# Seven half-size products in place of eight for the down projections of two feed-forward blocks, and the first weight slabs among the sums of the first norm

## The chip, the cores and the metric

The kernel is one program on one NeuronCore of a Trainium2 chip. All data is f32. The metric is the device time of one launch in microseconds; the median of three runs is given. TensorE multiplies, VectorE and ScalarE work on the results, SyncE asks for the weights, and the four run in parallel, held in order by semaphores only.

## The reference

Two transformer blocks over 256 latent tokens beside 256 context tokens, width 1024. The first has window pooling, differential attention, a bidirectional RWKV recurrence and a mixture of 32 experts. The second has two layers, each an attention mixer and a SwiGLU feed-forward of width 2816. What the change touches is the last line of each layer, and the first lines of the first block:

```
s = silu(c); mod = s @ w_ada + b_ada            # 6 x 1024 rows: shift, scale, gate, twice
p = (rms_norm(x, norm1_g) * (1 + scale) + shift) @ w_in

def swiglu(h, w_gate_up, w_down):
    g, u = split(h @ w_gate_up, 2)               # h: tokens x 1024, g and u: tokens x 2816
    return (silu(g) * u) @ w_down                # w_down: 2816 x 1024
h_lat = h_lat + g_f * swiglu(modulate(h_lat, sh_f, sc_f), w_gate_up, w_down)
h_ctx = h_ctx + cg_f * swiglu(...)               # first of the two layers only
```

The first layer (named "f0" in the kernel) sends 512 tokens through its feed-forward, the second ("f1") 256.

## The kernel before, in words

**Layout.** Features lie on the 128 partitions, tokens along them: the residual `H` and the normed activations `A` are 8 tiles of 128 x 512. A product takes a 128 x 128 unit of weights as the stationary operand and streams tokens past it into one of 8 PSUM banks (`banks`, 128 x 512). Every f32 matmul leaves two records in the profile, so counts of records are twice the counts in the code.

**Weights.** SyncE (`straight`, L2189) copies the weight stream from HBM to a ring of six 1 MB tiles of 16 units. It asks for tile t once TensorE has finished with tile t - 6. TensorE waits for a tile when it takes its first unit (`unit`). The tables, the parameters and the tokens are asked for from ScalarE's queue.

**Feed-forward, gate and up (`ffn`).** Both halves of the weights and tokens are cut in two, and each of 22 hidden tiles is computed as seven half-size products of four matmuls (the Winograd form of Strassen's scheme), 28 matmuls of 128 x 256 in f0 and of 128 x 128 in f1. VectorE makes the four sums of weight blocks for the tile after (`weights_summed`: four operations of 128 x 512, two buffers `wsum`), the four sums of token blocks once (`tsums`), and combines the products; ScalarE copies and applies silu. After the last hidden tile TensorE waits for VectorE's last product with silu (L2163).

**Feed-forward, down (`ffn_down`).** Eight output tiles in order. Each is one PSUM group of 22 matmuls, over all tokens at once (512 columns in f0, 256 in f1), read straight from the ring and from `hid`. VectorE adds the finished bank to the residual (`residual`, L1931 and L1933 in f0, L1937 in f1).

**Norm (`norm`).** ScalarE squares the eight tiles of `H`, each once its residual is there (L1289). TensorE sums them over the partitions with a matrix of ones in four strips (L530), ScalarE takes the root, VectorE the reciprocal (L1599), TensorE spreads the result to all partitions, and VectorE multiplies (L1604 in the first norm, L1613 in later ones).

**Start.** ScalarE asks for the parameters, for `ident` and `ones`, for the tokens (2 MB, `x_in`) and for the other tables (1.5 MB, `tables_in`). SyncE starts the weights when the tokens are there. TensorE transposes the tokens, does norm n1, then the first eight modulation slabs (`modulation`: one 1 MB tile each, four matmuls of 128 x 32 by 128 x 512 in four column strips, eight records a slab), turns the result (`modulation_out`, L542), and VectorE makes the coefficients (L1581, L1590, L1593). ScalarE then applies them to the normed tiles (L1307), and the first projection follows tile by tile. Between the root of n1 and the slabs' copy ScalarE asks for two small tables, `sw` (1.2 MB) and `cnt` (0.6 MB).

## Time and profile before

| | us |
|---|---|
| median of 3 runs | 2477.55 (2477.21 to 2479.27) |
| the profiled execution | 2481.53 |
| its span | 2479.7 |
| TensorE busy | 2315.2 (93% of the span) |
| VectorE busy | 909.7 (37%) |
| ScalarE busy | 497.2 (20%) |
| mean granted TensorE clock | 0.963 of full speed |

The span runs from the first to the last instruction that the profiler shows; the execution's own time is 1.8 us longer. In all rows times are in us from the span's start unless ns is written, "x" is a count of records, and what stands in square brackets is the idle time of that engine just ahead of the row, with what ended it.

### The profile page before, as it was taken

How to read it: one execution, taken by the hardware profiler on the slowest of the kernel's cores; microseconds unless marked ns; L12 is line 12 of the kernel's file. 1: busy time of each engine (PE TensorE's matmuls, PEld its weight loads, DVE VectorE, ACT ScalarE, POOL GpSimd, SP SyncE). 2: the span in 40 equal slices, each digit the busy share in tenths (PEclk: the TensorE clock that was granted, in tenths of full speed). 3: DMA queues.
4: the chain of work that ended last, by engine and by line, in shares of the span. 5: the costliest groups of instructions: out<-in, count | busy, mean ns of one | idle time of the engine just before them, and what ended most of it. 6: DMA issues, size and time to landing. Idle time of an engine off the chain costs nothing.

```text
span 2479.7 us, 40905 instructions
## 1 busy us (share of the span) xinstructions
PE 2315.2 (93%) x17296; PEld 1534.1 (62%) x17296; DVE 909.7 (37%) x1966; ACT 497.2 (20%) x1057; POOL 0.2 (0%) x4
## 2 busy tenths in 40 slices
PE   6999866999899899999999989999999999799998
PEld 3554415999788444444444437658888445688997
DVE  1047677444212221212123027444444001457731
ACT  3010342332002111111112026411010001251111
POOL 0000000000000000000000000000000000000000
PEclk8999987999899999999999999999999999999998
DMA  8253793000543699999982210012222122113431
GB/s 347 86 221 154 309 415 159 4 4 4 199 163 131 283 422 422 422 421 422 422 355 119 85 68 1 18 53 96 89 85 85 51 88 103 52 36 142 166 142 60
DMA packets 59638, 428.00 MB, mean 173 GB/s; under 512 B 6496, under 2 KB 7776, under 8 KB 8288
## 3 DMA queue, kind: packets, MB, share of 16 engines
q1 hardware_dynamic: 56880, 414.21, 42.2%
q10 hardware_dynamic: 2608, 11.58, 1.2%
q8 instruction: 120, 1.97, 0.3%
q14 instruction: 30, 0.25, 0.0%
HBM read 424.72 MB, written 1.05 MB: 172 GB/s over the span
## 4 chain that ended last, share of the span: by engine, by line
PE 89%; DVE 7%; ACT 1%; DMA 1%; issue 1%; ACTq 0%; DVEq 0%
PE bank L530 86%; PE bank L677 1%; DMA ring<-in_w 1%; DVE normed L1613 1%; DVE arena L1818 0%; ACT normed L1307 0%; DMA arena<-in_xin 0%; PE bank L1144 0%; DVE arena L1682 0%; DVE arena L1681 0%; DVE arena L1734 0%; PE bank L1153 0%; DVE arena L1830 0%; DVE arena L1829 0%; DVE small L1649 0%
## 5 line engine op out<-in xcount | busy, mean ns | idle before, releaser
L530 PE MATMUL bank<-arena 64*64 64x64 f32 (+8 forms) x8808 | 811.0, 291 | 22.2 <-DVEq L471 12.9
L530 PEld LDWEIGHTS bank<-arena 64*64 64x64 f32 (+4 forms) x8808 | 576.1, 150 | 212.2 <-issue 173.2
L530 PE MATMUL bank<-normed,ring 128*128 128x256 f32 (+2 forms) x1984 | 545.4, 432 | 15.2 <-DVE normed L1632 5.5
L530 PEld LDWEIGHTS bank<-normed,ring 128*128 128x128 f32 x1984 | 356.0, 195 | 192.9 <-issue 151.8
L530 PE MATMUL bank<-arena,ring 128*128 128x256 f32 (+2 forms) x1376 | 363.3, 420 | 4.6 <-DVE arena L2163 3.1
L530 PEld LDWEIGHTS bank<-arena,ring 128*128 128x128 f32 x1376 | 249.1, 190 | 111.3 <-issue 84.4
L530 PE MATMUL bank<-ring,arena 128*64 128x512 f32 (+1 forms) x1008 | 208.4, 611 | 6.2 <-DMA ring<-in_w 4.0
L530 PEld LDWEIGHTS bank<-ring,arena 128*64 128x64 f32 (+1 forms) x1008 | 62.8, 133 | 140.4 <-issue 120.8
L530 PE MATMUL bank<-ring,normed 128*32 128x512 f32 (+2 forms) x576 | 115.7, 606 | 19.9 <-DMA ring<-in_w 12.1
L1534 ACT ACTIVATE arena<-arena 128x256 f32<-128x256 f32 (+1 forms) x88 | 32.1, 365 | 341.4 <-DVE arena L2160 216.4
L2050 DVE TENSOR_TENSOR arena<-arena,bank 128x512 f32<-128x512 f32 x72 | 49.5, 688 | 136.9 <-PE bank L530 136.8
L530 PEld LDWEIGHTS bank<-ring,normed 128*32 128x32 f32 (+1 forms) x576 | 41.7, 141 | 80.9 <-issue 50.4
L1289 ACT ACTIVATE arena<-resid 128x512 f32<-128x512 f32 (+1 forms) x48 | 25.2, 524 | 322.8 <-DVE resid L1933 197.5
L1931 DVE SCALAR_TENSOR_TENSOR resid<-bank,mod2a,resid 128x256 f32<-128x256 f32 x16 | 7.7, 483 | 194.6 <-PE bank L530 194.6
L1334 ACT ACTIVATE arena<-bank,small 128x512 f32<-128x512 f32 (+1 forms) x112 | 69.1, 622 | 48.5 <-DVE small L1649 47.7
L1649 DVE TENSOR_REDUCE small<-bank 128x1 f32<-128x512 f32 (+1 forms) x112 | 63.8, 609 | 37.8 <-PE bank L530 37.7
L530 PE MATMUL bank<-arena,con 128*32 128x128 f32 (+6 forms) x640 | 68.7, 309 | 8.8 <-ACT arena L1289 3.4
L530 PEld LDWEIGHTS bank<-arena,con 128*32 128x32 f32 (+2 forms) x640 | 42.2, 138 | 37.6 <-issue 22.0
L530 PE MATMUL bank<-normed,arena 128*128 128x256 f32 (+1 forms) x352 | 64.8, 327 | 0.0
L1868 DVE TENSOR_TENSOR arena<-arena,bank 128x256 f32<-128x256 f32 x80 | 33.7, 421 | 79.9 <-PE bank L530 79.8
L1315 ACT ACTIVATE arena<-bank 128x512 f32<-128x512 f32 (+1 forms) x38 | 19.3, 508 | 207.5 <-PE bank L530 207.5
L530 PE MATMUL bank<-arena,sw 128*64 128x128 f32 (+4 forms) x288 | 50.5, 393 | 9.2 <-DVE arena L2095 9.2
(309 smaller groups left out, 1663.8 us busy)
## 6 DMA issues: line engine op xcount, KB each, us to landing
ring<-in_w SPq DMA_DIRECT2D x296, 1024.0 KB, 7.9
arena<-in_w SPq DMA_DIRECT2D x99, 1024.0 KB, 11.3
arena<-in_xin ACTq DMA_DIRECT2D x1, 2048.0 KB, 8.3
arena<-in_nab ACTq DMA_DIRECT2D x1, 2048.0 KB, 11.4
con<-in_con ACTq DMA_DIRECT2D x1, 1472.5 KB, 11.3
sw<-in_sw ACTq DMA_DIRECT2D x1, 1280.0 KB, 5.8
sw<-in_sw ACTq DMA_DIRECT2D x1, 1168.0 KB, 8.4
normed<-in_xin ACTq DMA_DIRECT2D x1, 1024.0 KB, 5.7
```

The costliest lines, as they stand in the source:

```text
L530: return nc.tensor.matmul(o, l, r, start=start, stop=stop, **kw)
L677: last = nc.tensor.transpose(banks[j[0]][:, c * P:(c + 1) * P], it["p"][x][:, c * P:(c + 1) * P], ident)
L1289: a.signals(f(sq[:, k, 0:n], H[:, k, cols], ACT.Square), "squared_" + name)
L1315: a.given(f(o, view(b, o), ACT.Copy, scale=scale))
L1334: a.given(f(it["p"][x][:, 0:it["nk"]], b[:, 0:it["nk"]], ACT.Exp, bias=it["nm"][:, x:x + 1], accum_out=it["den"][:, x:x + 1]))
L1534: f(z[:, half, :], z[:, half, :], ACT.Silu).then_inc(S("gate_silu_" + name), 1)
L1613: ins = tt(A[:, k, cols], H[:, k, cols], spread[:, 0:n], MUL)
L1649: ins = V.tensor_reduce(nm[:, x:x + 1], b[:, 0:nk], AX, MAX, negate=True)
L1868: v.gives(tt(SC[d]["Pt"], SC[d]["Pt"], j4(b, 256), ADD))
L1931: stt(out=H[:, k, 0:CTX], in0=b[:, 0:CTX], scalar=m[:, c + 1:c + 2], in1=H[:, k, 0:CTX], op0=MUL, op1=ADD)
L2050: v.given(tt(y, y, b[:, :], ADD))
```

## The change

The down product is cut as gate and up already are. The 22 hidden tiles are two halves of 11, the tokens two halves, and two output tiles form a pair, so a pair is a 2 x 2 block product done as seven products over 11 hidden tiles instead of eight. The 11 are taken in three parts of 4, 4 and 3 (`DOWN`), each with its own 1 MB weight tile (12 tiles a block, where there were 11; the last of three is padded); the seven sums stay open in seven banks over the three parts. VectorE makes the weight sums of every part, the sums of hidden blocks in the first pair (`hidden_summed`), and from the seven banks of a pair the four residual additions (`add_pair`). The norms behind both blocks wait for pairs, and put their squares into `A`.

At the start, five of the eight modulation slabs are put among the strips' sums of n1, behind its tiles 1, 3, 5, 6 and 7 (`first_slab`); the wait for the tables moves behind the first projections; and the tables, `cnt` and `sw` are asked for behind the copy of the modulation rows.

```diff
+FH = FT // 2
+DOWN = [range(lo, min(lo + 4, FH)) for lo in range(0, FH, 4)]
+N_FFN = FT * 2 * KD + KD // 2 * len(DOWN) * UPT
...
+        hsums = {n: [region(o, FH * n // 2, "p (f t) -> p f t", f=FH) for o in (11264, 14080, 22528)] for n in (T, SEQ)}
+        usums = {n: [region(16896 + n // 2 * i, n // 2) for i in range(5)] for n in (T, SEQ)}
...
                 for k in range(KD):
                     pe.wait_ge(S("squared_" + name), k + 1)
                     last = sums(k, (2, 3) if halves else range(4))
-                done(j, last)
+                    if k == KD - 1:
+                        done(j, last)
+                    if each is not None:
+                        each(k)
...
             def ffn_down(n, name):
-                marks["res_" + name] = dict(gave)
-                for m in range(KD):
-                    j = job("dve")
-                    for f in range(FT):
-                        last = mm(banks[j[0]][:, 0:n], unit(), hid[:, f, 0:n], f == 0, f == FT - 1)
-                    done(j, last)
+
+                q = n // 2
+                marks["down_" + name] = []
+                x11, x21, t3, x22 = (lambda k, lo=lo, c=c: hid[:, lo + k, c * q:(c + 1) * q]
+                                     for lo, c in ((0, 0), (FH, 0), (0, 1), (FH, 1)))
+                t1, t2, t4 = (lambda k, z=z: z[:, k, :] for z in hsums[n])
+                tile = FT
+                for m in range(KD // 2):
+                    js = [None] * 7
+                    for part, ks in enumerate(DOWN):
+                        w = unit(UPT)
+                        final = part == len(DOWN) - 1
+                        if final:
+                            st["free"][-1] = st["n"] + 7
+                        a = lambda i, h, k: w[:, (8 * i + 4 * h + k) * P:(8 * i + 4 * h + k + 1) * P]
+                        s1, s2, s3, s4 = (lambda k, z=z: z[:, k * P:(k + 1) * P] for z in wsum[tile % 2])
+                        for x, (l, r, weights, tokens) in enumerate((
+                                (lambda k: a(0, 0, k), x11, 0, 0), (lambda k: a(0, 1, k), x21, 0, 0), (s4, x22, 3, 0),
+                                (s2, t2, 1, 2), (s3, t3, 2, 3), (s1, t1, 1, 1), (lambda k: a(1, 1, k), t4, 0, 4))):
+                            if part == 0:
+                                js[x] = job("dve")
+                            if weights:
+                                pe.wait_ge(S("weights_summed_" + name), 3 * tile + weights)
+                            if tokens and m == 0:
+                                pe.wait_ge(S("hidden_summed_" + name), 4 * part + tokens)
+                            for k in ks:
+                                last = mm(banks[js[x][0]][:, 0:q], l(k - ks[0]), r(k), k == 0, k == FH - 1)
+                            if final:
+                                done(js[x], last)
+                        if not final:
+                            last.then_inc(full, 1)
+                            st["n"] += 1
+                        marks["down_" + name].append(st["n"])
+                        tile += 1
...
             transposes_in(xtok, None, "x_in")
-            norm("n1", sq_t, slice(0, T))
-            pe.wait_ge(S("silu_c"), 1)
             st["banks"] = 7
-            for x in range(KD):
+
+            def first_slab(k):
+
+                if k in (1, 3, 5, 6, 7):
+                    y = {1: 0, 3: 1, 5: 2, 6: 3, 7: 4}[k]
+                    if y == 0:
+                        pe.wait_ge(S("silu_c"), 1)
+                    modulation(y, ADA, cond1)
+
+            norm("n1", sq_t, slice(0, T), each=first_slab)
+            for x in range(5, KD):
                 modulation(x, ADA, cond1)
             modulation_out()
             st["banks"] = 8
-            pe.wait_ge(S("tables_in"), 16)
             marks["proj1"] = dict(gave)
             project(4, LAT, "act", "n1")
...
             st["banks"] = 7
+            pe.wait_ge(S("tables_in"), 16)
...
-            norm("n5", sq_b, slice(0, T))
+            norm("n5", A, slice(0, T))
...
             act.dma_start(arena[:, ATT:ATT + 4096], dram["xin"]).then_inc(S("x_in"), 16)
-            act.dma_start(con[:, 2 * P:CONST_W], dram["con"][:, 2 * P:CONST_W]).then_inc(S("tables_in"), 16)
             act.wait_ge(S("params_in"), 32)
...
+                    if pairs:
+                        act.wait_ge(S("pair_added_" + pairs), k // 2 + 1)
...
             norm("n1", sq_t, slice(0, T))
-            act.dma_start(sw[:, 0:SW1_W], dram["sw1"]).then_inc(S("small_in"), 16)
-            act.dma_start(region(16640, 1280), dram["cnt"]).then_inc(S("counts_in"), 16)
             act.wait_ge(back["dve"], marks["spread_n1"])
             modulation(KD - 1)
+            act.dma_start(region(16640, 1280), dram["cnt"]).then_inc(S("counts_in"), 16)
+            act.dma_start(con[:, 2 * P:CONST_W], dram["con"][:, 2 * P:CONST_W]).then_inc(S("tables_in"), 16)
+            act.dma_start(sw[:, 0:SW1_W], dram["sw1"]).then_inc(S("small_in"), 16)
             act.wait_ge(S("coef_n1"), 1)
...
-            norm("n5", sq_b, slice(0, T), after="res_f0")
+            norm("n5", A, slice(0, T), pairs="f0")
...
+            def hidden_summed(n, name, ks):
+
+                q = n // 2
+                ks = slice(ks[0], ks[-1] + 1)
+                rest = slice(FH + ks.start, FH + ks.stop)
+                t1, t2, t4 = (z[:, ks, :] for z in hsums[n])
+                x11, x12, x21, x22 = (hid[:, r, c * q:(c + 1) * q] for r in (ks, rest) for c in range(2))
+                v.signals(tt(t1, x12, x11, SUB), "hidden_summed_" + name)
+                v.signals(tt(t2, x22, t1, SUB), "hidden_summed_" + name)
+                v.signals(tt(x12, x22, x12, SUB), "hidden_summed_" + name)
+                v.signals(tt(t4, t2, x21, SUB), "hidden_summed_" + name)
+
+            def add_pair(n, name, m, mod):
+
+                q = n // 2
+                u1, u2, u6, u3, u4 = usums[n]
+                got = lambda: v.take()[:, 0:q]
+
+                def add(i, c, z):
+                    k = 2 * m + i
+                    cols = slice(T - n + c * q, T - n + (c + 1) * q)
+                    at = 80 + 2 * k + (1 if n == T and c == 0 else 0)
+                    return stt(out=H[:, k, cols], in0=z, scalar=mod[:, at:at + 1], in1=H[:, k, cols], op0=MUL, op1=ADD)
+
+                v.gives(V.tensor_copy(u1, got()))
+                v.gives(tt(u2, u1, got(), ADD))
+                v.gives(tt(u6, u1, got(), ADD))
+                add(0, 0, u2)
+                b = got()
+                tt(u3, u1, b, ADD)
+                v.gives(tt(u6, u6, b, ADD))
+                v.gives(tt(u4, u3, got(), ADD))
+                b = got()
+                v.does(tt(u6, u6, b, ADD))
+                v.gives(tt(u3, u4, b, ADD))
+                add(0, 1, u6)
+                add(1, 1, u3)
+                v.gives(tt(u1, u4, got(), SUB))
+                v.signals(add(1, 0, u1), "pair_added_" + name)
+
+            def down(n, name, mod):
+
+                dve.wait_ge(S("hidden_" + name), FT)
+                done = marks["down_" + name]
+                parts = len(DOWN)
+                for d in range(KD // 2 * parts):
+                    if d < parts:
+                        hidden_summed(n, name, DOWN[d])
+                    if d + 1 < KD // 2 * parts:
+                        if d > 0:
+                            dve.wait_ge(full, done[d - 1])
+                        weights_summed(name, FT + d + 1, 0)
+                        weights_summed(name, FT + d + 1, 1)
+                    if d % parts == parts - 1:
+                        add_pair(n, name, d // parts, mod)
...
-                    if m < FT - 1:
-                        weights_summed(name, m + 1, 0)
+                    weights_summed(name, m + 1, 0)
...
-                residual(mod, 5, slice(T - n, T))
+                down(n, name, mod)
```

Left out are the same edits for the second block, its norm n7, and the packing of the weights.

## Rows read from the trace of the kernel before

**Rows 1.** The page: the chain that ended last, by engine.
```profile
PE 89%; DVE 7%; ACT 1%; DMA 1%; issue 1%; ACTq 0%; DVEq 0%
```
**Rows 2.** Chain in order of time: start, length, what; the longest wait for weights.
```profile
303.39 13.28 DMA ring<-in_w
```
**Rows 3.** Windows: stretch, length, busy PE, PEld, DVE, ACT, POOL, clock, DMA share, GB/s.
```profile
2248.60:2385.00 136.40, 135.98 (x1216) 135.86 (x1216) 101.73 (x216) 17.01 (x65) 0.00 (x0) 1.00 0.45 163
...
1927.60:2078.00 150.40, 150.40 (x351) 66.69 (x352) 6.12 (x14) 5.01 (x9) 0.00 (x0) 1.00 0.18 69
```
**Rows 4.** Timeline, f0 gate and up, last two tiles: start, length, engine, line, operation.
```profile
1904.82 5.34 PE L530 MATMUL bank<-arena 128*128 128x256 f32 x24
...
1913.72 0.42 DVE L2160 TENSOR_TENSOR arena<-arena,bank 128x256 f32<-128x256 f32 x1 [0.98 <-PE bank L530]
...
1916.91 5.34 PE L530 MATMUL bank<-arena 128*128 128x256 f32 x24
...
1925.81 0.42 DVE L2160 TENSOR_TENSOR arena<-arena,bank 128x256 f32<-128x256 f32 x1 [2.38 <-PE bank L530]
```
**Rows 5.** Timeline, f0 down: residual of the last output tile, last square.
```profile
2078.91 0.48 DVE L1931 SCALAR_TENSOR_TENSOR resid<-bank,mod2a,resid 128x256 f32<-128x256 f32 x1 [18.01 <-PE bank L530]
...
2079.87 0.63 ACT L1289 ACTIVATE arena<-resid 128x512 f32<-128x512 f32 x1 [18.25 <-DVE resid L1933]
```
**Rows 6.** Timeline, f1 gate and up: two tiles, and the last one.
```profile
2355.39 2.84 PE L530 MATMUL bank<-arena 128*128 128x128 f32 x24
...
2357.78 0.69 DVE L2119 TENSOR_TENSOR arena<-arena,ring 128x512 f32<-128x512 f32 x1
...
2360.62 0.29 DVE L2160 TENSOR_TENSOR arena<-arena,bank 128x128 f32<-128x128 f32 x1
...
2361.65 2.84 PE L530 MATMUL bank<-arena 128*128 128x128 f32 x24
...
2380.41 2.84 PE L530 MATMUL bank<-arena 128*128 128x128 f32 x24
...
2385.15 0.29 DVE L2160 TENSOR_TENSOR arena<-arena,bank 128x128 f32<-128x128 f32 x1 [1.11 <-PE bank L530]
```
**Rows 7.** Timeline, f1 down: last residual and last square.
```profile
2462.64 0.48 DVE L1937 SCALAR_TENSOR_TENSOR resid<-bank,mod2b,resid 128x256 f32<-128x256 f32 x1 [9.01 <-PE bank L530]
2463.21 0.42 ACT L1289 ACTIVATE arena<-resid 128x256 f32<-128x256 f32 x1 [9.08 <-DVE resid L1937]
```
**Rows 8.** Timeline, f0: one sum of token blocks over four tiles of 256.
```profile
1661.64 1.23 DVE L2141 TENSOR_TENSOR arena<-normed,arena 128x1024 f32<-128x1024 f32 x1
```
**Rows 9.** Timeline of the start: transposes, squares of n1, sums, spread, slabs, coefficients.
```profile
10.13 6.39 PE L576 MATMUL bank<-con,arena 128*128 128x128 f32 x32 [10.13 <-DMA arena<-in_xin]
...
18.64 5.25 ACT L1289 ACTIVATE arena<-resid 128x512 f32<-128x512 f32 x8
...
19.39 5.21 PE L530 MATMUL bank<-arena,con 128*32 128x128 f32 x64 [2.87 <-ACT arena L1289]
...
26.24 2.07 PE L530 MATMUL bank<-rs_t,con 128*128 128x128 f32 x8 [1.64 <-DVE rs_t L1599]
...
28.25 5.88 PE L530 MATMUL bank<-ring,arena 128*32 128x512 f32 x48
28.42 4.87 DVE L1604 TENSOR_TENSOR normed<-resid,bank 128x512 f32<-128x512 f32 x8 [2.23 <-PE bank L530]
...
40.09 1.93 PE L530 MATMUL bank<-ring,arena 128*32 128x512 f32 x8 [0.55 <-DMA ring<-in_w]
...
44.03 0.19 DVE L1581 TENSOR_TENSOR mod<-bank,par 128x32 f32<-128x32 f32 x1 [10.73 <-PE bank L542]
...
44.80 9.00 ACT L1307 ACTIVATE normed<-normed,mod,coef 128x256 f32<-128x256 f32 x16 [2.05 <-DVE small L1609]
```
**Rows 10.** Windows of 1 us at the start (columns as in the third group).
```profile
22.00:23.00 1.00, 0.99 (x16) 0.35 (x16) 0.00 (x0) 0.97 (x2) 0.00 (x0) 0.50 1.03 434
...
29.00:30.00 1.00, 1.00 (x12) 0.32 (x8) 1.00 (x3) 0.00 (x0) 0.00 (x0) 0.82 1.02 418
```

More of the change, by code:

```diff
@@ L138 @@
 N_EVEN = 12 * KD + 32
-N_FFN = FT * 2 * KD + KD * FT
+FH = FT // 2
+DOWN = [range(lo, min(lo + 4, FH)) for lo in range(0, FH, 4)]
+N_FFN = FT * 2 * KD + KD // 2 * len(DOWN) * UPT
 N_ODD = 10 * KD
@@ L577, in transposes_in, with norm @@
                     done(j, last)
-            def norm(name, sq, cols, halves=False, between=None):
+            def norm(name, sq, cols, halves=False, between=None, each=None):
                 marks[name] = dict(gave)
@@ L1251, in _ @@
             ffn(SEQ, "f1", "n6")
-            norm("n7", sq_b, LAT)
+            norm("n7", A, LAT)
             for k in range(KD):
@@ L1272, in _, with norm @@
             act.dma_start(arena[:, ATT:ATT + 4096], dram["xin"]).then_inc(S("x_in"), 16)
-            act.dma_start(con[:, 2 * P:CONST_W], dram["con"][:, 2 * P:CONST_W]).then_inc(S("tables_in"), 16)
             act.wait_ge(S("params_in"), 32)
-            def norm(name, sq, cols, after=None, halves=False):
+            def norm(name, sq, cols, after=None, halves=False, pairs=None):
                 n = cols.stop - cols.start
@@ L1548, in _ @@
             ffn(SEQ, "f1")
-            norm("n7", sq_b, LAT, after="res_f1")
+            norm("n7", A, LAT, pairs="f1")
             modulate("n7", LAT, None)
@@ L2156, in ffn @@
                     v.gives(tt(z[:, 3, :], z[:, 5, :], b[:, q:n], ADD))
-                    if m < FT - 1:
-                        weights_summed(name, m + 1, 1)
+                    weights_summed(name, m + 1, 1)
                     b = v.take()
@@ L2278, in ffn @@
             out += [a[f], b[f]]
-        return out + [units(g["ffn_w_down_2"][l])]
+        dn = units(g["ffn_w_down_2"][l]).reshape(KD, 2, FH, P, P)
+        for m in range(KD // 2):
+            for ks in DOWN:
+                tile = np.zeros((2, 2, 4, P, P), np.float32)
+                tile[:, :, 0:len(ks)] = dn[2 * m:2 * m + 2, :, ks.start:ks.stop]
+                out.append(tile.reshape(UPT, P, P))
+        return out
     ev = g["even_w_in_2"][0]
```

## The prediction

> **What bounds the kernel now.** I read the chain of waits by engine first: TensorE is 89% of it, transfers 1% [rows 1]. So a change pays where it takes columns or waits from TensorE, and costs where TensorE is made to wait. Next come the windows over the stages touched: in the down stage of f0 and in gate and up of f1 TensorE is busy all but 0.3% of the time at a granted clock of 1.00 (2.4 GHz), and the weights need 0.18 and 0.45 of the DMA engines [rows 3]. Both are columns through TensorE and nothing else. The start is another matter: there the timeline shows TensorE waiting for tokens, squares, a reciprocal and weights in turn [rows 9], and the DMA engines full at a clock of 0.50 (1.2 GHz) [rows 10].
>
> **Down product of f0.** Before: 351 records in 150.4 us, 0.4285 each, so 352 take 150.8 us [rows 3]. After: a pair of output tiles has 7 products of 11 matmuls, 77 matmuls, and four pairs have 308, or 616 records of 256 columns. The gate and up stage runs just this form, with the same weight sums beside it: one tile of 28 matmuls goes from 1904.82 to 1916.91, 12.09 us [rows 4]. 308 matmuls are 11 such tiles: 133.0 us. **Gain 17.8.**
>
> **Down product of f1.** Before: eight output tiles at 9.01 + 0.48 = 9.49 us, 75.9 us [rows 7]. After: 11 times the tile of 2355.39 to 2361.65, 6.26 us, is 68.9 us [rows 6]. **Gain 7.0**, less than the eighth of 75.9 (9.5), because narrow matmuls run at 6.26 / 56 = 111.8 ns a record where 128 columns should take half of 215.9, the f0 pitch. The Trainium skill ("TensorE: Matmul & The Clock Gate", section "Wait — 56ns, not 53.3ns?") has a fixed 2.5 ns on each matmul whatever its width; over the 106.7 ns of two passes that would be 109.2 a record and 67.3 us, 1.6 us better than the trace. This trace does not agree (111.8 ns), and the row stands in the sum.
>
> **VectorE beside it.** Does it keep up? A part costs four weight sums at 0.72 each with the gap (0.69 busy) [rows 6], 2.9 us. In f1 the first pair also makes four hidden sums a part, of 512 elements twice and 384 once, at most 0.72 each: 8.1 us or so in all. Additions of a pair are 13 operations: nine of 128 columns at 0.29 [rows 6] and four residual ones, not seen at this width, between 0.29 and the 0.48 of 256 columns [rows 7]; I take 0.33, nearer the same width, and get 4.4 us with the gaps. TensorE needs 6.26 + 6.26 + 4.70 = 17.2 us for a pair, VectorE 8.7 + 4.4 = 13.1, and 21 in the first pair, because it starts with TensorE. I walked the first pair: the hidden sums of parts 0, 1 and 2 end 2.9, 8.7 and 13.9 us in, where the seventh products ask for them at 5.4, 11.6 and 16.5; the weight sums of parts 1, 2 and 3 end at 5.8, 11.6 and 16.8, and are asked for at 8.0, 13.9 and 19.0. The closest is about 2 us. Banks: seven of eight stay open, and the second product of the next pair needs the first of this one, which VectorE gives back with its first addition at 17.1, asked for at 18.1. That is the thinnest cover, 1 us; gone, it costs what it is late, once. So no wait: 0, at most 3. In f0 TensorE's parts are twice as long, and a hidden sum is 1.23 [rows 8]: the first pair is 33 us of TensorE against about 29 of VectorE, cost 0.
>
> **What is queued behind the new waits.** VectorE waits for the end of part d - 1 before it sums for part d + 1, and the additions of the pair stand behind this. That end is past whenever TensorE is in part d, so it delays additions only. SyncE has 12 tiles to ask for where it had 11, at 6.26 us a tile in f1 and a share of 0.45 as in gate and up [rows 3]: nothing.
>
> **Last tile of gate and up.** It now carries the weight sums of the first part. In f1 the next to last addition (L2160) stood 5.23 us after its tile's group began where sums were made, and 4.74 where they were not [rows 6]: **0.5 lost**. In f0 both stand at 8.90 [rows 4]: 0.
>
> **End of each down stage.** Three things grow. (1) Behind the sixth product VectorE has four operations: in f0 2 x 0.42 + 2 x 0.48 [rows 4, 5] and gaps, 1.9 us, and the seventh product (six records, 1.3 us) ends 0.6 earlier; in f1 1.3 against 0.67, 0.65. (2) Behind the seventh: a subtraction and an addition, in f0 0.42 + 0.48 + gap against 0.96 before to the square [rows 5], nothing; in f1 0.29 + 0.33 + gap against 0.48 [rows 7], 0.2. (3) Squares of two tiles wait for the last pair, where there was one: 0.63 and a gap in f0 [rows 5], 0.42 and a gap in f1 [rows 7]. **1.3 lost in f0, 1.3 in f1**; bounds 0.6 each if ScalarE and VectorE overlap better, 3 each if the four residual additions are slow.
>
> **The start.** Before: the last slab starts at 40.09, ends at 42.02, and the coefficients let ScalarE go at 44.80 [rows 9]. After, by the same rows: squares come every 0.66 us from 18.64, the sum of tile 1 ends at 20.5, and a slab at 1.2 GHz takes 1.94: 22.4. Two sums (a quarter of a slab's columns each, 0.49): 23.4. Now the clock. In the rows TensorE took up dense work with the spread at 26.24, and the clock rose at about 29.36 [rows 9, 10]; while it only kept pace with the squares, from 19.39 to 24.6, it stayed at 0.50 [rows 10]. The slabs make the stretch from 20.05 dense, so I let it rise at 23.3. From there a slab is 0.98 (5.88 / 6) and a sum 0.25: slab 24.4, slab 25.9, slab 27.1, last sum 27.3. The root and reciprocal took 24.60 to 26.24, so 28.9, with the fifth slab inside; the spread, half of 2.07, 30.0; slabs 5 to 7, 32.9. VectorE's eight multiplications (4.87) end at 35.0, a little behind the copy and turn of the rows (2.01 before, 34.9), and coefficients take 0.77: ScalarE goes at 35.8. **Gain 9.0.**
> The other end: with the clock at 1.2 GHz all along, the same walk gives 43.7, a gain of 1.1. The best end adds what the tokens land earlier without the tables beside them, 0 to 0.9; I take 0. Weights: eight tiles of 1.05 MB at 418 GB/s take 20 us, from 10.1 to 30.1 [rows 9, 10], asked for in time, since slab 1 ends at 24.4, and the eighth is needed at 31.9. The three table requests sit in the 2.05 us in which ScalarE waited for the coefficients [rows 9]; nobody reads the tables until the first projections are done. The projection stays paced by ScalarE's 9.00.
>
> **Sum.** -17.8 - 7.0 + 0.5 + 1.3 + 1.3 - 9.0 = -30.7 us. Span 2479.7 - 30.7 = 2449.0, profiled execution 2481.5 - 30.7 = 2450.8. It lay 4.0 above the median, 2477.55, from which the same difference gives **2446.9**.
>
> **Rivals.**
> *Clock stays low at the start.* The gain is 1.1 and the time 2454.8. For it: no rise from 19.39 to 24.6 with TensorE 0.99 busy in a window [rows 10]. Against: those records only kept pace with the squares, where slabs follow without a gap. 15%.
> *The start is given back.* Before 303.39 TensorE waits 13.28 us for weights [rows 2]. Were that stream timed by an absolute start, the 9.0 would vanish into it: 2455.9. Against: a tile is asked for when TensorE frees one, so the stream moves with TensorE. 10%.
> *VectorE late in the first pairs and at the ends.* The 1 us cover of the banks fails, and both ends take 3: 0.5 + 3 + 3 + 3 more than none, against 3.1 counted: 2453.3. 10%.
> *Sums in series (the other side).* If in every part TensorE had to wait for VectorE's weight sums, made only after the part before, 24 parts would lose 2.9 us each: +69.6, time 2516.5. It decides from a loss of 30.7 / 24 = 1.3 us a part. For it: VectorE does wait for part d - 1. Against: there are two buffers, and gate and up runs the same sums with TensorE idle 0.3% [rows 3]. 3%.
>
> **How the numbers follow.** The forecast has 62%, with its own range 2444 to 2450 (tokens 0.9 earlier and ends 0.6 each; clock up 2 us later, 1 us more at the ends). The range, 2443 to 2456, takes in the three milder rivals. Under 0.2% (5 us) from 2477.55 the measurement can't tell from no change. All cases but the last gain over 20 us: faster 0.96, same 0.01, slower 0.03.
>
> **What would show it.** Right: down of f0 in 133 us and of f1 in 69, with TensorE idle under 1 us in each; squares of two tiles one behind the other at their ends; the coefficients' ScalarE row at about 36, with the clock at 1.00 from about 24. Wrong: waits of TensorE for VectorE's sums or returned banks; a clock of 0.50 beyond 28; a wait for weights before the last slabs; the first wait for weights near 300 longer by what the start gained.

## The result and the profile after

| | before | after |
|---|---|---|
| median, same chip | 2478.41 (4 runs, 2477.21 to 2481.95) | 2452.31 (4 runs, 2448.7 to 2456.46) |
| profiled execution | 2481.53 | 2456.46, the slowest of its four |
| its span | 2479.7 | 2454.7 |
| TensorE busy | 2315.2 | 2289.6 |
| VectorE busy | 909.7 | 1021.5 |

The ratio is 0.989 (0.9878 to 0.9902): 26.1 us faster, where 30.7 were predicted. The forecast, 2446.9, is 5.4 below the median. The median lies outside the forecast's own range (2444 to 2450) and inside the wide one (2443 to 2456), which was drawn to take in three rivals.

The page of the kernel after, busy time by engine and the chain by engine (for [rows 1]):
```profile
PE 2289.6 (93%) x17824; PEld 1585.7 (65%) x17824; DVE 1021.5 (42%) x2166; ACT 495.5 (20%) x1057; POOL 0.2 (0%) x4
PE 88%; DVE 8%; DMA 2%; ACT 1%; issue 1%; ACTq 0%; DVEq 0%
```
The chain in order of time, after, the two down stages: start, length, what.
```profile
1922.23 131.94 PE bank L534 x610
...
2367.14 68.40 PE bank L534 x610
```
Each down stage is one piece: 610 of 616 records with nothing between them. The timeline shows the two ends (for [rows 5] and [rows 7]) with the strips' sums of the next norm behind the last product, and in f1 the last tile of gate and up and the first additions (for [rows 6]). f0:
```profile
2055.38 1.52 PE L534 MATMUL bank<-normed,con 128*32 128x128 f32 x48
...
2057.01 1.29 ACT L1333 ACTIVATE normed<-resid 128x512 f32<-128x512 f32 x2 [31.95 <-DVE resid L2196]
...
2059.37 0.95 DVE L1644 RECIPROCAL rs_t<-rs_t 128x128 f32<-128x128 f32 x1 [2.25 <-ACT rs_t L1335]
```
f1:
```profile
2360.71 2.84 PE L534 MATMUL bank<-arena 128*128 128x128 f32 x24
...
2365.92 0.29 DVE L2259 TENSOR_TENSOR arena<-arena,bank 128x128 f32<-128x128 f32 x1
...
2383.64 0.29 DVE L2198 COPY arena<-bank 128x128 f32<-128x128 f32 x1
...
2387.21 0.35 DVE L2196 SCALAR_TENSOR_TENSOR resid<-arena,mod2b,resid 128x128 f32<-128x128 f32 x1
...
2439.34 0.55 DVE L1644 RECIPROCAL rs_t<-rs_t 128x64 f32<-128x64 f32 x1 [1.87 <-ACT rs_t L1335]
```
The timeline of the start (for [rows 9]):
```profile
10.62 5.03 PE L580 MATMUL bank<-con,arena 128*128 128x128 f32 x32 [10.62 <-DMA arena<-in_xin]
...
17.92 5.24 ACT L1333 ACTIVATE arena<-resid 128x512 f32<-128x512 f32 x8
...
27.74 1.16 PE L534 MATMUL bank<-rs_t,con 128*128 128x128 f32 x8 [0.78 <-DVE rs_t L1644]
29.00 4.87 DVE L1649 TENSOR_TENSOR normed<-resid,bank 128x512 f32<-128x512 f32 x8 [1.32 <-PE bank L534]
29.06 1.07 PE L534 MATMUL bank<-ring,arena 128*32 128x512 f32 x8 [0.17 <-DMA ring<-in_w]
...
31.53 1.07 PE L534 MATMUL bank<-ring,arena 128*32 128x512 f32 x8 [1.41 <-DMA ring<-in_w]
...
34.05 1.93 PE L534 MATMUL bank<-ring,arena 128*32 128x512 f32 x8 [1.45 <-DMA ring<-in_w]
36.13 0.60 ACT L1396 ACTIVATE rs_t<-bank 128x512 f32<-128x512 f32 x1 [9.53 <-PE bank L534]
...
38.77 8.96 ACT L1351 ACTIVATE normed<-normed,mod,coef 128x256 f32<-128x256 f32 x16 [2.04 <-DVE small L1654]
```
The last three slabs each wait for weights, and ScalarE goes at 38.77, not 35.8. The windows after, columns as in [rows 3]: between the tokens and the weights the DMA engines are all but idle, and at 34 the clock falls.
```profile
9.00:10.00 1.00, 0.00 (x0) 0.00 (x0) 0.00 (x0) 0.00 (x0) 0.00 (x0) 1.00 0.08 33
10.00:11.00 1.00, 0.38 (x2) 0.41 (x3) 0.00 (x0) 0.00 (x0) 0.00 (x0) 1.00 0.00 0
11.00:12.00 1.00, 1.00 (x7) 1.00 (x6) 0.00 (x0) 0.25 (x1) 0.00 (x0) 1.00 0.36 82
12.00:13.00 1.00, 1.00 (x7) 1.00 (x6) 0.00 (x0) 0.74 (x2) 0.00 (x0) 1.00 0.76 270
...
23.00:24.00 1.00, 1.00 (x24) 0.88 (x20) 0.00 (x0) 0.16 (x1) 0.00 (x0) 0.68 0.95 401
...
34.00:35.00 1.00, 0.95 (x8) 0.20 (x8) 0.00 (x0) 0.00 (x0) 0.00 (x0) 0.50 1.01 418
...
2231.00:2232.00 1.00, 1.00 (x6) 1.00 (x6) 0.00 (x0) 0.00 (x0) 0.00 (x0) 0.50 0.00 0
```
By stages, read from the two timelines ("reciprocal" is that of the norm behind the stage):

| stretch | before | after | difference | predicted |
|---|---|---|---|---|
| start, to ScalarE's coefficients | 44.80 | 38.77 | -6.0 | -9.0 |
| from there to the f0 down stage | 1882.73 | 1883.46 | +0.7 | 0 |
| f0 down to reciprocal | 154.05 | 137.14 | -16.9 | -16.5 |
| from there to f1 gate and up | 167.44 | 167.43 | 0 | 0 |
| f1 gate and up | 137.34 | 140.34 | +3.0 | +0.5 |
| f1 down to reciprocal | 78.54 | 72.20 | -6.3 | -5.7 |
| rest of the span | 14.8 | 15.4 | +0.6 | 0 |
| span | 2479.7 | 2454.7 | -25.0 | -30.7 |

So 3.0 us are missing at the start, 2.5 in f1's gate and up, and 1.3 in stretches whose code is the same (0.6 of them is the last norm's spread and what follows: 1.71 for its eight records, 1.12 before). The down stages gave 1.0 more than predicted.

### The profile page after: what moved, and what is told of

Read it like the earlier page. It is cut to its first block, busy times and chain, and to the rows that moved or that the text cites. A ratio compares the mean times of both kernels' runs of the same rounds, so it can differ in the third digit from the quotient of the medians.

```text
span 2454.7 us, 42278 instructions
## 1 busy us (share of the span) xinstructions
PE 2289.6 (93%) x17824; PEld 1585.7 (65%) x17824; DVE 1021.5 (42%) x2166; ACT 495.5 (20%) x1057; POOL 0.2 (0%) x4
## 3 DMA queue, kind: packets, MB, share of 16 engines
HBM read 426.81 MB, written 1.05 MB: 174 GB/s over the span
## 4 chain that ended last, share of the span: by engine, by line
PE 88%; DVE 8%; DMA 2%; ACT 1%; issue 1%; ACTq 0%; DVEq 0%
PE bank L534 85%; PE bank L684 2%; DMA ring<-in_w 1%; DVE normed L1658 1%; DVE arena L1863 0%; ACT normed L1351 0%; DMA arena<-in_xin 0%; DVE normed L1677 0%; PE bank L1187 0%; DVE arena L1726 0%; DVE arena L1727 0%; DVE arena L1779 0%; PE bank L1196 0%; DVE arena L1874 0%; DVE arena L1875 0%
## 5 line engine op out<-in xcount | busy, mean ns | idle before, releaser
L534 PE MATMUL bank<-arena 64*64 64x64 f32 (+8 forms) x9512 | 934.5, 294 | 24.2 <-DVEq L475 14.6
L534 PEld LDWEIGHTS bank<-arena 64*64 64x64 f32 (+4 forms) x9512 | 686.5, 154 | 224.2 <-issue 177.4
L534 PE MATMUL bank<-normed,ring 128*128 128x256 f32 (+2 forms) x1984 | 546.2, 432 | 15.4 <-DVE normed L1677 5.5
L534 PE MATMUL bank<-arena,ring 128*128 128x256 f32 (+1 forms) x1200 | 226.6, 341 | 5.1 <-DVE arena L2262 3.6
L534 PEld LDWEIGHTS bank<-arena,ring 128*128 128x128 f32 x1200 | 196.1, 191 | 25.8 <-DVE arena L2262 4.2
L534 PE MATMUL bank<-ring,normed 128*32 128x512 f32 (+2 forms) x576 | 118.8, 627 | 20.3 <-DMA ring<-in_w 12.4
L2163 DVE TENSOR_TENSOR arena<-ring 128x512 f32<-128x512 f32 x68 | 47.1, 692 | 65.6 <-issue 52.8
L534 PE MATMUL bank<-arena,con 128*32 128x128 f32 (+5 forms) x512 | 63.3, 312 | 11.6 <-DVE arena L2023 5.0
L534 PEld LDWEIGHTS bank<-arena,con 128*32 128x32 f32 (+1 forms) x512 | 40.2, 145 | 39.1 <-issue 26.0
L2251 DVE TENSOR_TENSOR arena<-arena,bank 128x512 f32<-128x512 f32 (+1 forms) x44 | 24.4, 554 | 93.3 <-PE bank L534 93.3
```

The lines of the kernel that those rows point to most:

```text
L534: return nc.tensor.matmul(o, l, r, start=start, stop=stop, **kw)
L2163: v.does(tt(s1, a21, a22, ADD))
L2251: v.gives(tt(z[:, 0:5:4, :], p1, two(b), ADD))
```

## The experiments

Eleven kernels, timed beside the kernel before on the same chip. The first three ask whether the gain is the sum of two parts, and what chance moves.

**The down products alone.** The slabs, `each=`, the tables, `cnt`, `sw` and the wait for the tables stay where the kernel before has them.
```diff
+            norm("n1", sq_t, slice(0, T))
+            pe.wait_ge(S("silu_c"), 1)
...
-            norm("n1", sq_t, slice(0, T), each=first_slab)
-            for x in range(5, KD):
+            for x in range(KD):
...
```


> The kernel with the new down products alone; the start is that of before. The changed kernel's trace gives the down stages -16.9 us in f0 and -6.3 in f1 from the last hidden tile to the reciprocal, and about +0.5 in gate and up of f1: -22.7 against the kernel before. Rival (the down products slow something else, as the 3.0 us that gate and up of f1 lost in that trace would have it): -20.

Measured: 2455.78, ratio 0.9903 (0.9889 to 0.9918), -24.1 us. f0 takes 137.14 from down to reciprocal and f1 72.20, as in after, and f1's gate and up 137.82.

**The start alone**: the kernel before, with the new order of the slabs and the tables.
```diff
...
-            norm("n1", sq_t, slice(0, T))
-            pe.wait_ge(S("silu_c"), 1)
...
-            for x in range(KD):
...
+            norm("n1", sq_t, slice(0, T), each=first_slab)
+            for x in range(5, KD):
...
```

> The kernel before with the new start alone (slabs among the sums of n1, tables asked for behind the rows). ScalarE should go at about 38.8 us as in the changed kernel, and the time be 6.0 us under the kernel before if the start's gain is kept to the end. Rival (given back in the stretch near 300 us where TensorE waits for weights): 0 to -2.

Measured: 2474.6, 0.9973 (0.9963 to 0.9983), -5.3 between the medians, 6.7 by the ratio. ScalarE goes at 39.53, 5.3 earlier than before, and f0's down stage starts 7.3 earlier (2.1 of that lie in a stretch of the same code, see under "Not foreseen" below): nothing is given back. The parts add up: 24.1 + 5.3 = 29.4, and the kernel with both gained 28.7 on that chip, next.

**The changed kernel again**, unedited.

> The changed kernel unaltered, for a second trace and a tighter time: 26 us under the kernel before. If the 2.5 us that the first tile of gate and up of f1 lost at 1.2 GHz belongs to the change, it is there again; if it is where the clock happens to rise, this trace shows it elsewhere or not at all.

Measured: 2451.2, 0.9884 (0.987 to 0.9898), -28.7. ScalarE goes at 39.05. f1's gate and up took 137.83, where the first profile had 140.34. The code is the same; what differs is the clock in which the stage begins. This window of the repeated kernel, as its stage starts, stands against 2231:2232 above:
```profile
2223.00:2224.00 1.00, 0.50 (x4) 0.31 (x3) 0.96 (x2) 1.00 (x1) 0.00 (x0) 0.95 0.00 0
```
Here the clock is 0.95 at once; there it was 0.50 until 2232. That is the 2.5 us. Both occur with the same code, so the change alone does not set it: of the eleven traces here with the new down products, four have the long stage (139.8 to 140.3) and seven the short one (137.8).

**The start: why 38.8 and not 35.8.** Two theories: the weights are late because the DMA engines lie idle from the tokens on (mine), or the tables' move is what counts. First, **the tokens in SyncE's queue**, straight ahead of the weights:
```diff
-            act.dma_start(arena[:, ATT:ATT + 4096], dram["xin"]).then_inc(S("x_in"), 16)
...
-            sp.wait_ge(S("x_in"), 16)
+            sp.dma_start(arena[:, ATT:ATT + 4096], dram["xin"]).then_inc(S("x_in"), 16)
```


> The changed kernel, with the tokens asked for from SyncE's queue just ahead of the weights, and no wait between them. Theory (the last three slabs wait for their weights, which start 10.5 us in): the weights follow the tokens without a gap, the eighth tile lands 2 to 3 us earlier, ScalarE goes at 36 to 37 instead of 38.8, and the time is 2 to 3 us under the changed kernel. Rival (the start hangs on the clock and the squares): no change of the eighth slab, 0 us. Side effect possible: the tokens land later by up to 1 us if the weights take bandwidth from them.

Measured: 2453.52, 0.9884 (0.987 to 0.9898). Timeline of this kernel:
```profile
12.25 6.15 PE L580 MATMUL bank<-con,arena 128*128 128x128 f32 x32 [12.25 <-DMA con<-in_con]
...
30.88 2.97 PE L534 MATMUL bank<-ring,arena 128*32 128x512 f32 x24
36.01 0.60 ACT L1395 ACTIVATE rs_t<-bank 128x512 f32<-128x512 f32 x1 [7.36 <-DVE normed L1648]
```
The slabs hardly wait for weights any more (24 records without a gap, 2.97 us), but `ident` and `ones` now share the DMA engines with the tokens and the 1 MB tiles. The view of the DMA issues gives them 11.0 us from issue to landing (last number):
```profile
con<-in_con ACTq DMA_DIRECT2D x1, 128.0 KB, 11.0
```
Before it was 2.5. The transposes start 1.6 later, and ScalarE goes at 38.19: hardly better, where 36 to 37 was expected. Its copy of the rows, at 36.01, is released by VectorE and not by the last slab.

**The first six tiles in ScalarE's queue, behind the tokens.**
```diff
+            for t in range(RING):
+                act.dma_start(ring[:, t * TILE:(t + 1) * TILE], dram["w"][t]).then_inc(ring_full[t], 16)
...
-            sp.wait_ge(S("x_in"), 16)
-            straight(0, middle)
+            straight(RING, middle)
```


> The changed kernel, with the first six weight tiles asked for on ScalarE's queue directly behind the tokens, SyncE starting with the seventh. Theory (the DMA engines lie empty from about 9.1 to 12.5 us, between the tokens and the first weights, and the last three slabs pay for it): the hole closes, tokens still land near 10.5 us because the weights stand behind them in one queue, no slab waits over 0.3 us, ScalarE goes at 35 to 36 instead of 38.8 to 39.1, and the time is 3 us under the changed kernel. Rival (the hole is no cause, the DMA engines' order is): the last slab still ends near 36 and nothing is gained.

Measured: 2452.57, 0.9889 (0.9871 to 0.9906). Window, then timeline of this kernel:
```profile
10.00:11.00 1.00, 0.02 (x1) 0.05 (x1) 0.00 (x0) 0.00 (x0) 0.00 (x0) 1.00 0.97 410
```
```profile
28.99 0.95 DVE L1646 RECIPROCAL rs_t<-rs_t 128x128 f32<-128x128 f32 x1 [27.09 <-ACT rs_t L1337]
...
31.08 2.78 PE L534 MATMUL bank<-ring,arena 128*32 128x512 f32 x24
31.26 4.87 DVE L1651 TENSOR_TENSOR normed<-resid,bank 128x512 f32<-128x512 f32 x8 [1.32 <-PE bank L534]
...
36.22 0.60 ACT L1398 ACTIVATE rs_t<-bank 128x512 f32<-128x512 f32 x1 [7.36 <-DVE normed L1651]
...
38.86 8.96 ACT L1353 ACTIVATE normed<-normed,mod,coef 128x256 f32<-128x256 f32 x16 [2.05 <-DVE small L1656]
```
The hole is closed (0.97 against 0.00), and the slabs end at 33.9 instead of 36.0, but ScalarE goes at 38.86 all the same. Its copy of the rows starts at 36.22, released not by TensorE but by VectorE's eighth multiplication: `act.wait_ge(back["dve"], marks["spread_n1"])` stands ahead of it. In after the multiplications had ended at 33.87, 2.1 before the last slab; here they end at 36.13, because the reciprocal came at 28.99 and not at 26.73. The clock was at 0.50 until 26 in this trace. So this run shows that there is a second wait, and that it binds when the reciprocal is late; it does not show what closing the hole is worth with an early one.

**The tables early again.** Only their request goes back to its place behind the tokens.
```diff
             act.dma_start(arena[:, ATT:ATT + 4096], dram["xin"]).then_inc(S("x_in"), 16)
+            act.dma_start(con[:, 2 * P:CONST_W], dram["con"][:, 2 * P:CONST_W]).then_inc(S("tables_in"), 16)
...
-            act.dma_start(con[:, 2 * P:CONST_W], dram["con"][:, 2 * P:CONST_W]).then_inc(S("tables_in"), 16)
```


> The changed kernel, with the 1.5 MB of tables asked for right behind the tokens as in the kernel before; cnt and sw stay behind the modulation rows. Theory (the tables ran in the hole that otherwise lies empty while the first weights are on their way): ScalarE goes within 0.5 us of 38.9, time as the changed kernel. Rival (the prediction's sum, every byte ahead of the eighth tile delays it): the eighth tile lands 2.6 us later, ScalarE goes at 41.5, time +2.6.

Measured: 2450.3, 0.9888 (0.9871 to 0.9904). Window and timeline:
```profile
10.00:11.00 1.00, 0.66 (x3) 0.69 (x4) 0.00 (x0) 0.00 (x0) 0.00 (x0) 1.00 0.99 424
```
```profile
34.43 1.07 PE L534 MATMUL bank<-ring,arena 128*32 128x512 f32 x8 [1.42 <-DMA ring<-in_w]
...
38.28 8.97 ACT L1352 ACTIVATE normed<-normed,mod,coef 128x256 f32<-128x256 f32 x16 [2.04 <-DVE small L1654]
```
With the tables in the hole, the eighth tile lands at 34.43, against 34.05 with the hole empty. The 1.5 MB ran in time that was idle, so moving them away bought next to nothing.

**The slabs behind the norm, the tables late**: what the move of the tables is worth alone.
```diff
+            norm("n1", sq_t, slice(0, T))
+            pe.wait_ge(S("silu_c"), 1)
...
-            norm("n1", sq_t, slice(0, T), each=first_slab)
-            for x in range(5, KD):
+            for x in range(KD):
...
```


> The changed kernel, with all eight slabs again behind n1, the tables still asked for late: it tells what the interleaving alone is worth. Theory: the seventh tile can be asked for only after slab 0 ends near 29 us and lands about 5 us later with nothing else in the queues, so the last slab ends near 37 to 38 and ScalarE goes at 40 to 41: interleaving is worth about 1.5 us, the move of sw and cnt the other 4. Rival (the order alone is the gain): ScalarE goes at 44.

Measured: 2454.52, 0.9899 (0.9882 to 0.9915); its profiled execution was its slowest. Window and timeline:
```profile
28.00:29.00 1.00, 1.00 (x9) 0.78 (x12) 0.00 (x0) 0.00 (x0) 0.00 (x0) 0.50 0.00 0
```
```profile
39.96 1.94 PE L534 MATMUL bank<-ring,arena 128*32 128x512 f32 x8 [2.84 <-DMA ring<-in_w]
...
44.69 8.96 ACT L1343 ACTIVATE normed<-normed,mod,coef 128x256 f32<-128x256 f32 x16 [2.05 <-DVE small L1646]
```
ScalarE goes at 44.69. The two traces with the start of before have 44.80 (before) and 43.64 (the down products alone), so the rival was right, not my theory (40 to 41). The six tiles of the ring land early, then the DMA engines idle (0.00) until slab 0 frees a buffer. In these traces the whole gain at the start is the slabs' new place.

**VectorE's weight sums late**, the side on which the change would lose. VectorE waits for TensorE's end of part d, no longer of d - 1, before it sums for d + 1.
```diff
-                        if d > 0:
-                            dve.wait_ge(full, done[d - 1])
+                        dve.wait_ge(full, done[d])
```


> The changed kernel, with VectorE waiting for the end of part d, not d - 1, before it sums for part d + 1, as with a single buffer. The prediction's rival priced this at 2.9 us a part, +69.6 us. Counting that each part's first two products (3.45 us in f0, 1.79 in f1) need no sums: nothing in f0's inner parts, 1.1 us in each of f1's, and at the three pair ends the bank that the second product needs, 1.7 us in f0 and 2.4 in f1, with 2 us more in f1's first pair for the hidden sums: about +6 in f0 and +17 in f1, +23 us in all.

Measured: 2486.94, 1.0029 (1.0018 to 1.0039): 8.2 slower than before, some 35 more than after. TensorE's waits in this kernel, f0's down stage and then f1's: who waits for whom, us in total, times, the longest.
```profile
PE bank L534 <- DVE arena L2198: 5.2, 3, 2.0
PE bank L534 <- DVE arena L2168: 1.2, 4, 0.3
```
```profile
PE bank L534 <- DVE arena L2168: 10.6, 8, 1.6
PE bank L534 <- DVE arena L2198: 7.0, 3, 2.3
```
From down to reciprocal f0 takes 146.8 (+9.6) and f1 97.2 (+25.0). The expectation, +23, was too low by a third. In f1, where 17 was expected and 25 came, the clock fell behind the waits: the granted clock was 0.73 and 0.84 from 2396 to 2404, and 0.70 and 0.87 from 2444 to 2452 (means of 4 us each). The mechanism of the fourth rival exists and is large enough to turn the sign; the second buffer of sums is what keeps it away.

**Both waits of the start gone**: the tiles in ScalarE's queue, and no wait for VectorE ahead of the copy; the slabs' own signal covers what the copy reads.
```diff
-            act.wait_ge(back["dve"], marks["spread_n1"])
```


> As the kernel with the first weights on ScalarE's queue, and ScalarE no longer waits for VectorE's eight multiplications of n1 before it copies the modulation rows (the copy's own wait, for the last slab, already lies behind the spread). Theory (with the weights in time, the copy waits 2 us for VectorE, and turn and coefficients stand behind it): ScalarE goes 0.8 us after the multiplications end instead of 2.7, at 36.9 if the clock is as late as in that trace, 34.5 to 37 in general; time 2 us under it. Rival (weights or clock bind there too): no change, 38.9.

Measured: 2447.77, 0.9877 (0.9861 to 0.9894).
```profile
30.99 4.87 DVE L1650 TENSOR_TENSOR normed<-resid,bank 128x512 f32<-128x512 f32 x8 [1.32 <-PE bank L534]
...
33.72 0.60 ACT L1398 ACTIVATE rs_t<-bank 128x512 f32<-128x512 f32 x1 [5.14 <-PE bank L534]
...
35.90 0.19 DVE L1627 TENSOR_TENSOR mod<-bank,par 128x32 f32<-128x32 f32 x1
36.66 8.96 ACT L1353 ACTIVATE normed<-normed,mod,coef 128x256 f32<-128x256 f32 x16 [2.35 <-DVE small L1655]
```
Here is the walk of the prediction: slabs, copy and turn lie beside VectorE's multiplications, which end last (35.86), and ScalarE goes at 36.66 (predicted 35.8). The reciprocal, at 28.72, is as late as in the kernel with only the queue changed (28.99), so the two compare: 2.2 us for the second wait. The times alone do not separate them: the ratios differ by 0.0012, and their intervals overlap.

**And the squares one by one**: on top, VectorE signals tile 2m of a pair when its last addition is done.
```diff
-                        act.wait_ge(S("pair_added_" + pairs), k // 2 + 1)
+                        act.wait_ge(S("pair_added_" + pairs), k + 1)
...
-                add(0, 1, u6)
+                add(0, 1, u6).then_inc(S("pair_added_" + name), 1)
+                v.own["pair_added_" + name] = v.own.get("pair_added_" + name, 0) + 1
```


> The same, and the even tile of each pair signals its residual by itself, so that ScalarE squares it before the pair's end. Theory (squares of two tiles stand one behind the other at the ends): from the last product to the reciprocal 0.5 us less in f0 and 0.4 in f1, 0.9 in all; the whole is the fastest kernel, 27 to 29 us under the kernel before... with the start's gain. Rival (the spread of the norm hangs on VectorE's last addition alone): 0.

Measured: 2447.33, 0.9871 (0.9854 to 0.9887), the lowest median of all. f0's end:
```profile
2053.92 0.63 ACT L1335 ACTIVATE normed<-resid 128x512 f32<-128x512 f32 x1 [31.36 <-DVE resid L2197]
...
2055.16 0.63 ACT L1335 ACTIVATE normed<-resid 128x512 f32<-128x512 f32 x1 [0.61 <-DVE resid L2197]
```
The first square stands beside the last addition. Down to reciprocal is 136.47 in f0 (-0.7) and 71.76 in f1 (-0.4). The medians with and without this edit are 0.4 apart: too little for the timing to show, the stage lengths show it.

**The copy's wait gone without the queue**: the weights in SyncE's queue again, on top of the tables early, with the signals for each tile as well.
```diff
-            act.wait_ge(back["dve"], marks["spread_n1"])
...
-                        act.wait_ge(S("pair_added_" + pairs), k // 2 + 1)
+                        act.wait_ge(S("pair_added_" + pairs), k + 1)
...
-                add(0, 1, u6)
+                add(0, 1, u6).then_inc(S("pair_added_" + name), 1)
+                v.own["pair_added_" + name] = v.own.get("pair_added_" + name, 0) + 1
```

> The changed kernel with the tables right behind the tokens, the copy of the rows not waiting, and the even tiles' own signals. Theory (here the weights of the last slab still land near 34.4 us, 0.1 behind the end of the multiplications): ScalarE goes at 37.8 to 38.3, no more than 0.5 us earlier than with the tables early alone, since the copy waits for the last slab, and 0.9 us are gained at the ends. Rival (the copy's wait for VectorE binds here too): 36.

Measured: 2450.39, 0.9891 (0.9874 to 0.9907). The last slab starts at 34.43 and ScalarE goes at 38.27, as with the tables early alone. Taking away one of the two waits leaves ScalarE's start at 38.2 to 38.9 in three traces; with neither taken away it is 38.1 to 39.5 in five; taking away both gives 36.66, and 35.34 in the kernel with the signals, whose start is the same code. As long as the weights are late, the wait for VectorE costs at most 0.2 us (the late-sums kernel, whose last slab ended at 35.61 and whose multiplications ended at 35.80). With the weights in time it bound in both traces that keep it, and in both the reciprocal was late (28.78 and 28.99). With after's reciprocal the copy would start near 33.96, and 2.2 to 2.6 behind it ScalarE would go at 36.1 to 36.6 without touching the second wait: an estimate, which no trace here tests.

## Why the prediction was right, and where it fell short

**Down of f0: right.** TensorE takes 133.15 us, from 1922.23 to 2055.38 (predicted 133.0 and 11 tiles of 12.09). The new stage was read off a stage of the same form, cover included, and no price per instruction was needed.

**Down of f1: right.** 69.0 us, predicted 68.9; 68.40 / 610 is 112.1 ns a record. By the 2.5 ns of the Trainium skill ("TensorE: Matmul & The Clock Gate", section "Wait — 56ns, not 53.3ns?"), taken once a record, it would have been 67.3 by estimate; the trace still does not agree at this width.

**VectorE beside it: right.** The first bank was given back at 2383.64 + 0.29, so the copy began 16.5 into the stage (predicted: given back at 17.1, asked for at 18.1). No wait followed. A residual addition of 128 columns took 0.35 (0.33 taken). That the cover can fail is shown by the late sums.

**Last tile of gate and up: right.** 2365.92 - 2360.71 is 5.21 where 5.23 was read; the stage is 0.5 longer than before in the seven traces whose clock was up at its start.

**Ends: right in f0, too dear in f1.** Columns and ends together gained 16.9 in f0 (16.5) and 6.3 in f1 (5.7). From the last product to the reciprocal before took 2.78 in f0 and 2.37 in f1, after 3.99 and 3.22: 1.2 and 0.85 lost, where 1.3 each was predicted. The two squares stand together at 2057.01, 1.29 long, as foretold. Signals per tile give 0.7 and 0.4 of that back.

**The start: wrong by 3.0.** Two steps failed.
The step "eight tiles of 1.05 MB at 418 GB/s take 20 us, from 10.1 to 30.1". The eighth tile came at 34.05. The queue had been full from 10 on in the trace of before only because the tables were in it. These rows of before say so, columns as in [rows 10]:
```profile
10.00:11.00 1.00, 0.87 (x4) 0.90 (x5) 0.00 (x0) 0.00 (x0) 0.00 (x0) 1.00 1.10 471
11.00:12.00 1.00, 1.00 (x7) 1.00 (x6) 0.00 (x0) 0.60 (x1) 0.00 (x0) 1.00 1.02 436
```
I took the rate of a full queue for one that the change itself empties. Tiles land 2.5 apart (31.53, 34.05), so 20 us was right for the eight and the start of the stream was not: the DMA engines are full from 13 on, at 0.99. In the kernel with the signals, where the hole is closed, the eighth tile lands 2.1 earlier:
```profile
31.96 1.06 PE L534 MATMUL bank<-ring,arena 128*32 128x512 f32 x8 [0.80 <-DMA ring<-in_w]
```
The other 1.9 up to 30.1 are there with the hole closed too, and no run separates them. The stall also let the clock fall: the last slab took 1.93 and not 1.07, the turn of the rows 1.11 and not the 0.66 of the traces with the clock up.
The step "copy and turn in parallel" with VectorE's multiplications. ScalarE waits for the last of them before it copies. In after this cost nothing, since the multiplications ended at 33.87 and the last slab at 35.98. With the weights in time and the clock late, it cost 2.2 (38.86 against 36.66). Put right in the prediction's own walk, the copy starts at 35.0 and ScalarE goes at 37.8 instead of 35.8, an estimate from the 2.01 and 0.77 used there. The line stands in the code of before and I had not read it as a wait that would come last.

The clock step hit by luck: in after it rose in the window 23:24 (0.68, predicted 23.3). The start of four kernels is the same code, and the other three did otherwise. In the repeated kernel and the start alone the granted clock stayed at 1.00 from 9 to 31, and in the kernel with the late sums it was 0.50 from 19 to 25. The walk also had the first slab at the low clock, where in after the clock was still 1.00 until 20. The reciprocal was done at 27.7 there (predicted 28.9), at 26.6 and 27.1 in the two without a low stretch, and at 29.6 with the late sums:
```profile
28.66 0.95 DVE L1644 RECIPROCAL rs_t<-rs_t 128x128 f32<-128x128 f32 x1 [26.76 <-ACT rs_t L1335]
```
ScalarE went at 38.77, 39.05, 39.53 and 38.08 all the same: with the weights late, the clock of the norm decides next to nothing.

**Not foreseen: chance of some 5.5 us in one profile.** Whether f1's gate and up begins at 0.50 or near 1.00 differs between executions: 2.5 us. The stretch from 630 to f0's gate and up has the same code in all thirteen traces and comes in two lengths: 1027.3 to 1029.0 in eight, 1030.8 to 1031.2 in five. The four traces with the long gate and up of f1 (after, the tokens in SyncE's queue, the slabs behind the norm, and the one with rows and signals) are all among those five. So after's profile, the slowest of its four runs, carries 3.1 + 2.5 us that the repeated kernel's does not. In the table above, the +0.7 is therefore two opposites: 2.3 less than before up to 627, 3.0 more from there on. In the repeated kernel the same line reads 1880.68, 2.1 less than before. What one profile says of a microsecond or two outside the changed stages is chance of this size. I have not found what sets it.

**Rivals.** The reading under "given back" was wrong: the 13.28 of [rows 2] is the length of a piece of the chain that is given to a transfer, and TensorE's own waits for weights from 244 to 400 are 12.1 us in nine, the longest 3.0. After they are 12.4 in twelve, so nothing of the start's gain is lost there, and the start alone keeps its 5.3. "Clock low" fell: in all ten traces with slabs among the sums the clock was up by 26, though it fell again in the stalls behind. Of the signs named for being wrong, one came: waits for weights before the last slabs, and with them the 0.50 from 34 on. "VectorE late" fell. "Sums in series" is real, 35 us when forced rather than 69.6. The first two products of each part need no sums, so TensorE has work while VectorE makes them; the prediction's 2.9 a part had left that out.

## What to carry to other kernels

A transfer in front of the critical one may cost nothing, if it fills a time in which the queue would be empty; look at the DMA share window by window before moving it away. When a wait is predicted to go, list every wait of the same instruction and of the one behind it: of two that end close together (2.1 us apart in after, 0.2 in the late-sums kernel with the same start) the trace shows only the later one, and removing that one may bring nothing. A half-size product scheme can be priced from a stage that already has its form, as long as its sums have a second buffer.

## What the hardware did that I had not expected

- With the first tile asked for only when the tokens' landing had been signalled (10.5), the DMA engines' share was 0.08, 0.00, 0.36, 0.76 in the four windows from 9 to 13 us: about 3 us lost between two transfers.
- A transfer of 128 KB took 11.0 us instead of 2.5 when the tokens and 1 MB tiles were asked for in another queue at the same time.
- The same start code ran with no stretch at a clock of 0.50 in two traces, with one of 3 us in after and with one of over 6 us in the late-sums kernel. The reciprocal of n1 began between 25.67 and 28.66 in these four, which have the hole in the DMA queue, and between 26.99 and 28.99 in the six without it (one of them, the tokens in SyncE's queue, started 1.6 late). The ranges overlap, so these traces do not show that closing the hole delays the norm. One profile each doesn't show what sets the clock.
